# One transformer layer on one core: token sums by small products, tiles in other PSUM banks and another order of splits at the two stage changes

## The reference

```python
def rms_norm(x, g):
    xf = x.astype(jnp.float32)
    y = xf * lax.rsqrt(jnp.mean(xf * xf, axis=-1, keepdims=True) + EPS)
    return (y * g.astype(jnp.float32)).astype(x.dtype)

def modulate(h, shift, scale):
    return h * (1.0 + scale[:, None, :]) + shift[:, None, :]

        h = modulate(rms_norm(x, g_mix[i]), sh2, sc2)
        cq, ckv, kidx, widx, mq, mk, mv, ga, gb = split_cols(h @ w_in[i])
        ...
        h = modulate(rms_norm(x, g_ffn2[i]), sh3, sc3)
        x = x + 0.5 * (1.0 + gt3[:, None, :]) * swiglu(h, w1_ffn2[i], w3_ffn2[i], w2_ffn2[i])
```

## Time and profile before

| | |
|---|---|
| time, median of 3 runs | 1148.05 us (1146.92 to 1148.19) |
| profiled execution, its own time | 1148.91 us |
| its span in the profile | 1147.0 us |
| PE busy | 1121.8 us (98%) |
| DVE busy | 564.9 us (49%) |
| ACT busy | 502.2 us (44%) |
| POOL busy | 182.1 us (16%) |
| mean granted PE clock | 0.997 |

### The profile page before, as it was taken

One profiled execution on the slowest core, in us unless ns is written; L12 is line 12 of the kernel. 1 busy time (PEld: TensorE's weight loads), 2 busy tenths in 40 slices (PEclk: granted clock), 3 DMA queues, 4 the chain that ended last, 5 costly groups with the idle time before them and its releaser, 6 DMA issues.

```text
span 1147.0 us, 14769 instructions
## 1 busy us (share of the span) xinstructions
PE 1121.8 (98%) x5421; PEld 902.0 (79%) x5421; DVE 564.9 (49%) x912; ACT 502.2 (44%) x874; POOL 182.1 (16%) x114
## 2 busy tenths in 40 slices
PE   6999999999999999999999999999999999999998
PEld 4678888888888868877776778877888888888887
DVE  3544454444344475489884537677333333332232
ACT  4565646555444443244555654444232332232233
POOL 0055454454333510000000000040000000000000
PEclk9999999999999999999999999999999999999999
DMA  9846655665555333222212123322332332243221
GB/s 307 282 147 191 224 170 179 196 211 174 175 174 174 91 90 104 55 56 74 55 38 74 52 60 92 92 74 74 110 110 73 101 118 73 91 134 101 78 74 74
DMA packets 159099, 138.25 MB, mean 121 GB/s; under 512 B 3551, under 2 KB 157522, under 8 KB 159058
## 3 DMA queue, kind: packets, MB, share of 16 engines
q1 hardware_dynamic: 130948, 109.38, 30.7%
q10 hardware_dynamic: 28110, 28.32, 7.6%
HBM read 135.59 MB, written 2.10 MB: 120 GB/s over the span
## 4 chain that ended last, share of the span: by engine, by line
PE 86%; DVE 7%; SPq 3%; ACT 2%; DMA 1%; issue 1%; POOL 0%; ACTq 0%; DVEq 0%; POOLq 0%
PE ps L373 26%; PE ps L375 26%; PE ps L374 26%; SPq L926 2%; PE ps L1150 2%; PE ps L1177 2%; PE ps L1161 2%; DVE w_lo L352 2%; DVE score L1534 1%; DMA raw<-in_w_ffn 1%; DVE max L1532 1%; SPq L932 1%; DVE tmp L444 1%; ACT w_hi L347 1%; PE ps L500 1%
## 5 line engine op out<-in xcount | busy, mean ns | idle before, releaser
L352 DVE TENSOR_TENSOR w_lo<-raw,w_hi 128x1024 fp32r<-128x1024 f32 (+1 forms) x164 | 239.2, 1459 | 375.9 <-ACT w_hi L347 375.9
L373 PE MATMUL ps<-h_hi,w_hi 128*128 128x512 f32 x1008 | 400.6, 397 | 7.9 <-DVE w_lo L352 4.7
L375 PE MATMUL ps<-h_hi,w_lo 128*128 128x512 f32 x1008 | 393.7, 391 | 0.0
L374 PE MATMUL ps<-h_lo,w_hi 128*128 128x512 f32 x1008 | 393.0, 390 | 0.0
L347 ACT ACTIVATE w_hi<-raw 128x1024 fp32r<-128x1024 f32 (+1 forms) x164 | 183.5, 1120 | 362.1 <-PE ps L375 361.7
L373 PEld LDWEIGHTS ps<-h_hi,w_hi 128*128 128x128 f32 x1008 | 189.7, 188 | 54.8 <-issue 9.7
L375 PEld LDWEIGHTS ps<-h_hi,w_lo 128*128 128x128 f32 x1008 | 189.5, 188 | 40.9
L374 PEld LDWEIGHTS ps<-h_lo,w_hi 128*128 128x128 f32 x1008 | 189.9, 188 | 37.6 <-issue 0.2
L373 PE MATMUL ps<-g_hi,w_hi 128*128 128x512 f32 x330 | 129.9, 394 | 0.1
L375 PE MATMUL ps<-g_hi,w_lo 128*128 128x512 f32 x330 | 128.6, 390 | 0.0
L374 PE MATMUL ps<-g_lo,w_hi 128*128 128x512 f32 x330 | 128.5, 389 | 0.0
(11 more groups left out here) (217 smaller groups left out, 1010.6 us busy)
## 6 DMA issues: line engine op xcount, KB each, us to landing
raw<-in_w_ffn SPq DMA_DIRECT2D x42, 1024.0 KB, 5.4
ada<-in_w_ada ACTq DMA_DIRECT2D x27, 1024.0 KB, 5.1
raw<-in_w_ffn SPq DMA_DIRECT2D x16, 1408.0 KB, 6.3
raw<-in_w_in SPq DMA_DIRECT2D x64, 256.0 KB, 3.2
ada<-in_w_ada SPq DMA_DIRECT2D x16, 512.0 KB, 8.8
raw<-in_w_out SPq DMA_DIRECT2D x16, 256.0 KB, 3.0
x_tok<-in_x SPq DMA_DIRECT2D x4, 512.0 KB, 5.4
raw<-in_w_ffn SPq DMA_DIRECT2D x8, 256.0 KB, 7.3
```

The costliest lines, as they stand in the source:

```text
L352: nc.vector.tensor_tensor(tiles_of(w_lo[j % SPL], nk), raw_of(f, j, nk), tiles_of(w_hi[j % SPL], nk).bitcast(F32), ALU.subtract).then_inc( ...
L373: nc.tensor.matmul(ps[:, bank, :], hi, rhs_hi, start=start, stop=False)
L374: nc.tensor.matmul(ps[:, bank, :], hi, rhs_lo, start=False, stop=False)
L375: return nc.tensor.matmul(ps[:, bank, :], lo, rhs_hi, start=False, stop=stop)
```

## The change

It does five things, at both stage changes (n = 1 and n = 2).

1. The sums of squares are made token by token: `pe_token_sums` runs eight products of 128x1 (the partial sums as the stationary operand, a column of ones as the moving one), which leave 128x4 numbers. ACT takes their square root, DVE the reciprocal, and DVE spreads them over a diagonal of 128x512 (`dve_diag`). One product with ones (`pe_factors_and_shift`, one group later) makes the row of factors in PSUM bank 4. The scale of the mean, which stood in the squares, moves into the square root.
2. `dve_scaled` reads the factors from PSUM; a copy in `tmp[3]` (with `factor_done`) is made after the last `h_lo`, for `dve_unscale`. The copy of the shift moves there too.
3. The unscaled units go to banks 6 and 7 instead of 0 and 1. The fifth and sixth unit (banks 0 and 1) then no longer wait for the scaling. PE waits once more for the last reduction of the modulation (`ada_red`), which used these banks.
4. `pe_second_pair` runs k = 4 to 7 in blocks, too: four groups of the third unit, then four of the fourth.
5. The fifth unit's split stands at the end of `act_h` and `dve_h`, ahead of the scaling of the unscaled units. At n = 2 the sixth unit's split stands behind the first SiLU on ACT and behind the scaling on DVE.

The diff, cut to its core:

```diff
@@ -427,7 +428,7 @@
         def dve_scaled(n, k):
 
-            nc.vector.scalar_tensor_tensor(nrm[:, k % 4, :], tmp[:, 3, :] if n else ps[:, B_SUM, :], a_mul[:, n, k:k + 1], xT[:, k, :],
+            nc.vector.scalar_tensor_tensor(nrm[:, k % 4, :], ps[:, B_SUM, :], a_mul[:, n, k:k + 1], xT[:, k, :],
                                            ALU.mult, ALU.mult).then_inc(u_done, 1)
@@ -438,11 +439,9 @@
         def dve_h(dve, n, u):
 
-            dve.wait_ge(shift_psum, n)
-            nc.vector.tensor_copy(shift[:, :], ps[:, B_MOD, 0:2]).then_inc(shift_done, 1)
             dve.wait_ge(sqrt_done, n + 1)
-            nc.vector.reciprocal(tmp[:, 3, :], tmp[:, 3, :]).then_inc(rstd_done, 1)
-            dve.wait_ge(rstd_done, n + 1 + (2 if n == 2 else 0))
+            dve_diag(dve, tmp[:, 3, :], rtok[:, :], diag_done, n + 1 + (2 if n == 2 else 0))
+            dve.wait_ge(row_done, n + 1)
             dve_scaled(n, 0)
@@ -452,11 +451,16 @@
             dve_low(dve, n, KD - 1)
+            dve.wait_ge(shift_psum, n)
+            nc.vector.tensor_copy(shift[:, :], ps[:, B_MOD, 0:2]).then_inc(shift_done, 1)
+            nc.vector.tensor_copy(tmp[:, 3, :], ps[:, B_SUM, :]).then_inc(factor_done, 1)
+            lo_u(dve, u + 4)
+            dve.wait_ge(factor_done, n)
 
         def act_h(act, n, u):
 
             act.wait_ge(sum_done, n)
-            nc.scalar.activation(tmp[:, 3, :], ps[:, B_SUM, :], ACT.Sqrt, bias=eps[:, :]).then_inc(sqrt_done, 1)
+            nc.scalar.activation(rtok[:, :], ps[:, B_SUM, 0:QT], ACT.Sqrt, bias=eps[:, :], scale=1.0 / D_MODEL).then_inc(sqrt_done, 1)
@@ -471,6 +475,7 @@
                     hi_u(act, u + 3)
+            hi_u(act, u + 4)
@@ -522,12 +527,20 @@
-        def pe_sums_and_shift(pe, n):
+        def pe_token_sums(pe, n):
 
             pe.wait_ge(acc_done, 6 * n)
-            nc.tensor.matmul(ps[:, B_SUM, :], ones[:, :], tmp[:, 2, :], start=True, stop=False)
             pe.wait_ge(sq_done, KD * n)
-            nc.tensor.matmul(ps[:, B_SUM, :], ones[:, :], tmp[:, (KD - 1) % 2, :], start=False, stop=True).then_inc(sum_done, 1)
+            for t in range(QT):
+                nc.tensor.matmul(ps[:, B_SUM, t:t + 1], tmp[:, 2, t * P:(t + 1) * P], ones[:, 0:1], start=True, stop=False)
+                last = nc.tensor.matmul(ps[:, B_SUM, t:t + 1], tmp[:, (KD - 1) % 2, t * P:(t + 1) * P], ones[:, 0:1],
+                                        start=False, stop=True)
+            last.then_inc(sum_done, 1)
+
+        def pe_factors_and_shift(pe, n):
+
+            pe.wait_ge(diag_done, n + 1)
+            nc.tensor.matmul(ps[:, B_SUM, :], ones[:, :], tmp[:, 3, :], start=True, stop=True).then_inc(row_done, 1)
             pe.wait_ge(part_sum, 2 * n)
@@ -537,28 +550,30 @@
-            pe.wait_ge(x_done, KD * n + KD - 1)
+            pe.wait_ge(ada_red, 2 + (N_MOD * KD - ADA_FIRST) // 2)
...
-                    last = mm3(0, u, kk, y_hi[n][:, kk, :], y_lo[n][:, kk, :], kk == 0, kk == KD - 1)
+                    last = mm3(B_Y, u, kk, y_hi[n][:, kk, :], y_lo[n][:, kk, :], kk == 0, kk == KD - 1)
...
                 if kk == lag - 1:
-                    pe_sums_and_shift(pe, n)
+                    pe_token_sums(pe, n)
...
+                if kk == lag:
+                    pe_factors_and_shift(pe, n)
 
         def pe_second_pair(pe, n, u):
 
             half = KD // 2
-            order = [(q, k) for q in range(2) for k in range(half)] + [(q, k) for k in range(half, KD) for q in range(2)]
+            order = [(q, k0 + k) for k0 in (0, half) for q in range(2) for k in range(half)]
@@ -571,7 +586,7 @@
-                if j % 2 == 0:
+                if j % 2 == 0 and not (isinstance(i, int) and i == 1 and j == 0):
                     pe.wait_ge(g_done, KF * f + 2 * i + j // 2 + 1)
@@ -684,7 +701,11 @@
-            if not first and not unscaled:
+            if unscaled:
+                hi_u(act, U_UP[1] + 5)
+            elif f == 1 and isinstance(i, int) and i == 0:
+                pass
+            elif not first:
@@ -723,12 +744,13 @@
                 dve_unscale(dve, U_UP[1], (tmp[:, 0, :], tmp[:, 1, :]))
+                lo_u(dve, U_UP[1] + 5)
@@ -1040,7 +1062,7 @@
-                if u >= U_LAT + 4:
+                if u >= U_LAT + 6:
                     pe.wait_ge(evac, u - U_LAT - 3)
@@ -1307,7 +1329,7 @@
-                if q >= 2:
+                if q >= 3:
                     hi_u(act, u + 2)
@@ -1454,8 +1476,7 @@
-            for q in range(2, 4):
-                lo_u(dve, U_LAT + q + 2)
+            lo_u(dve, U_QKV + 1)
```

More of the change, by code:

```diff
@@ L173, in build_layer @@
         ps = ctx.enter_context(nc.psum_tensor("ps", [P, 8, SEQ], F32))
-        B_SUM, B_MOD, B_ADA = 4, 5, 6
+        B_SUM, B_MOD, B_ADA, B_Y = 4, 5, 6, 6
         U0_BANK = (6, 7, 2, 3)
@@ L225, in build_layer @@
         shift_done = sem("shift_done")
+        factor_done = sem("factor_done")
         const_done = sem("const_done")
@@ L388, in act_square @@
                 act.wait_ge(acc_done, 6 * (n - 1) + k - 1)
-            nc.scalar.activation(tmp[:, k % 2, :], xT[:, k, :], ACT.Square, scale=D_MODEL ** -0.5 if n < 3 else 1.0).then_inc(sq_done, 1)
+            nc.scalar.activation(tmp[:, k % 2, :], xT[:, k, :], ACT.Square).then_inc(sq_done, 1)
         def dve_square_sum(dve, n, k):
@@ L551, in pe_unscaled_pair @@
                     k = kk - lag
-                    last = mm3(1, u + 1, k, y_hi[n][:, k, :], y_lo[n][:, k, :], k == 0, k == KD - 1)
+                    last = mm3(B_Y + 1, u + 1, k, y_hi[n][:, k, :], y_lo[n][:, k, :], k == 0, k == KD - 1)
                     if k == KD - 1:
@@ L590, in pe_ffn @@
                 pe_second_pair(pe, 2, U_UP[f] + 2)
-            with pe.Fori(2 - f, KF // 2) as i:
+                for j in range(4):
+                    up(1, j)
+            with pe.Fori(2, KF // 2) as i:
                 for j in range(4):
@@ L717, in dve_unscale @@
                 dve.wait_ge(unit_done, done(u + q))
-                nc.vector.tensor_tensor(dst[q], ps[:, q, :], tmp[:, 3, :], ALU.mult).then_inc(y_scaled, 1)
+                nc.vector.tensor_tensor(dst[q], ps[:, B_Y + q, :], tmp[:, 3, :], ALU.mult).then_inc(y_scaled, 1)
         def dve_pair(dve, f, i, jp, nk):
@@ L730, in dve_pair @@
             else:
-                if not first:
+                if not first and not (f == 1 and isinstance(i, int) and i == 0):
                     for q in (2, 3):
```

## The result

| | before | after |
|---|---|---|
| time, median of 5 runs | 1148.11 us (1146.92 to 1148.37) | 1142.77 us (1141.8 to 1143.27) |
| span of the profiled execution | 1147.0 us | 1140.8 us |
| PE busy | 1121.8 us | 1120.4 us |
| ratio after / before | | 0.9943, 95% interval 0.9926 to 0.996 |

The changed kernel is 5.3 us faster by the medians, whose own ratio is 0.9953. By the ratio of the table it is 6.5 us faster, with an interval from 4.6 to 8.5.

A forecast was written before the change was run, and what follows sets the result against it. TensorE, busy 98% of the span, bounds the kernel, plus its stalls. Two stage changes of 25.4 us, 50.8 against 55.67, save 4.9: 1148.91 - 4.9 = 1144.0 profiled, median 1143.2 us, range 1141.8 to 1146.2.

The forecast's parts named there:

- Token sums: PE at each stage change: 16 records at 0.109 us make 1.74 us against 1.71 for two full-width sums, no gain.
- fourth rival: Small products last 0.25 us each and following products wait for the drain: slower, 1148.6 to 1150 us, chance 0.04.
- Factor: Square root, reciprocal, diagonal and row product at each stage change: scaling starts at 409.3, 1.7 us earlier.
- This wait takes the place of the reciprocal: Third tile's split waits until the first unscaled tile has ended, so the scaling chain gains only 0.3 us.
- The order in blocks: Third tile's second half runs in one block, giving the fifth tile's split 12 products (2.72 us) of cover.
- Early split ahead of scaling: Fifth tile's split precedes scaling on ACT and DVE; otherwise DVE would stand at the first tile's scaling and its copies first.
- Banks: Banks 6 and 7 free banks 0 and 1, so the fifth and sixth tiles need not wait for scaling; by themselves nothing.
- Stage time: From first unscaled product to fifth tile: 25.4 us at each stage change, together 50.8 against 55.67.
- Second rival: The wait moves to late h_lo at the third tile's last groups: 2 to 3 us gain, 1145 to 1146, chance 0.15.
- The sixth tile's split: On ACT and DVE after the first stage change: ready by 432.6, needed by PE at 433.2, margin 0.6 us.
- Profiled execution: Whole kernel: 1148.91 - 4.9 = 1144.0 us, lying 0.86 above the median, so median 1143.2.
- The first rival: The clock falls at one or both stage changes: 1144.9 us with one fall, 1146.6 with two, chance 0.12.

The follow-up runs named there:

- wide sums: Changed kernel with the full-width sums and the 128x512 square root and reciprocal, without row product and factor copy: 1144.08 us, ratio to before 0.9948.
- token sums only: Kernel before with only the token-by-token sums, the row product, the two later copies and the new ada wait: 1149.74 us, ratio to before 1.0002.
- old banks: Changed kernel with the unscaled tiles in banks 0 and 1 again and the waits that this needs: 1151.01 us, ratio to before 1.0014.
- alternating: Changed kernel, but the second half of the third and fourth tile alternates again as before: 1148.8 us, ratio to before 0.9997.
- late split: Changed kernel with the splits of the fifth and sixth tile behind the scaling again: 1148.65 us, ratio to before 0.9994.
- the kernel before with the sums apart: Kernel before with the latents' sums (24 records) cut into two halves, six full products between them: 1148.49 us, ratio to before 1.0.
- changed, sums apart: Changed kernel with the latents' sums cut into two halves, six full products between them: 1142.07 us, ratio to before 0.994.
- shift later: Changed kernel with the latents' sums in two halves and the small shift products moved to before the fourth tile: 1141.63 us, ratio to before 0.9937.
- idle filled: Kernel before with 8 and 10 unread 128x128 products where PE stands before the fifth tile: 1147.99 us, ratio to before 0.9989.

## Where the prediction was right, and the step that failed

The forecast was right in sign, and right in the mechanism at the two stage changes. It was wrong in the sum: it has no term for the clock. The gain forecast was 4.9 us. The stage times gave 4.67, and fewer clock falls gave the rest, up to 5.3 by the medians of the result, 6.2 by the spans of the two profiles and 6.5 by the ratio, which puts the time at 1141.5, below the range's low end. That the median (1142.77) still came within 0.4 us of 1143.2 is in part luck: the stage term was 0.2 us too large, and the clock term that was left out has the other sign. Step by step:

- *Token sums, "1.74 us against 1.71: nothing".* Measured 1.70. Right, and 0.109 per record holds for 32 in a row. So the fourth rival is out; its range of 1148.6 to 1150 did not follow from its own price either, at which a gain of 0.3 us was left, 1147.8.
- *Factor, "scaling starts 1.7 us earlier".* 1.73. Right.
- *"This wait takes the place of the reciprocal, and the scaling chain gains only 0.3 us".* 0.24. Right; "wide sums" and "token sums only" show it from both sides: 0.2 us at a stage change, or nothing over both.
- *"The order in blocks gives the split 12 products of cover".* Right: without it, 1.8 to 1.9 us at each change come back as the same wait of 1.79.
- *Early split ahead of scaling.* Right: 1.85 and 2.91 more without it.
- *Banks, "cost and give nothing by themselves. They free banks 0 and 1".* Right as a condition: with the old banks and the early split, PE waits 4.12 us for DVE. The banks alone, without the early split, were not run.
- *Stage time "25.4 us".* 25.53 and 25.47, so 4.67 us less where the sum has 4.9. The row product took 0.91, not 0.86, and the wait before the fourth tile was as forecast (0.29).
- *Second rival, "the wait moves" to the third tile's last groups.* It did not: in the trace after, PE is busy for all of 420 to 430 us.
- *"The sixth tile's split: ready by 432.6, PE needs it at 433.2".* It was ready at 433.38, since DVE's instruction took 2.13 us instead of 1.23. In the kernel before the same split took 1.77, too; in both, POOL runs an instruction of 128x512 beside it, and no run takes the two apart. PE needed the split at about 433.4 and went on at 433.44: the margin of 0.6 was used up, and next to nothing was lost.
- *"Profiled execution: 1148.91 - 4.9 = 1144.0. That execution lies 0.86 above the median of the runs".* This is the step that failed. The sum is made of stage times alone; it puts the change in the number of clock falls at nothing, and treats what lies between an execution and the median as a constant that both kernels share. But that distance depends on the number of falls, at 1.5 us each, and their number differs between the two kernels. The profiled execution of before had one fall, inside; the one of after had none and took 1142.77, not 1144.0. The difference of the spans, 6.15 us, is 4.67 of stage times and 1.5 of this fall. The earlier trace rows had its price already (at most 1.7); the prediction used it only against the change.
- *The first rival asked only whether the change adds a fall.* It adds none: in eight traces with the new sums no fall begins at them. It takes some away. The change puts in 1.7 us of small products and takes 1.8 and 2.3 us of idle PE out. In five traces ("alternating", "late split", "old banks", "token sums only" and the kernel before with the sums apart) a fall begins at such an idle stretch: once in its middle, three times within its last 0.5 us, once 0.5 us behind it. It does not come each time: of 13 such stretches of 1.7 to 4.1 us in seven traces, these five have a fall. The five traces of kernels without such a stretch (the changed kernel twice, "wide sums", "changed, sums apart", "shift later") have none at the stage changes, and "idle filled" shows that filling the stretches helps. The Trainium skill, "TensorE: Matmul & The Clock Gate", Part 1 (the HAM clock gate), says that the clock is set by how busy TensorE has been. The traces agree, as far as the falls begin at idle time or at long runs of small products. That the change also makes the fall behind the latents' sums rarer is not shown: the changed kernel's profiles have none there, but "wide sums", with nearly the same stage times, has one.

## What to carry to other kernels

Before a long instruction on a busy-looking engine is shortened, look for what ends the wait behind it: here a reciprocal of 3.35 us was worth 0.2, because the next split waited for a weight buffer that PE still held. Where two tiles share their product groups in turn, both end late; finishing one in a block lets its successor's preparation run under the other, but only if the preparation stands early enough in the helpers' queues and the target bank is free, and here the kernel with any one of these three taken out was no faster than before. Read the granted clock of every run before a median is taken for a sum of waits: in some executions an idle stretch costs 1.5 us more than it lasts. To check a sum of waits, compare the fastest runs of the two kernels, not only the medians: here they lie 4.66 us apart, and the stage times give 4.67.

## What the hardware showed beyond what was expected

The times of one kernel fall into steps of about 1.5 us, which go with mean granted clocks of 0.998, 0.997 and 0.995. In the traces a fall is a stretch of 3.4 us (in two places twice that, 6.8) at 1.2 GHz, and costs 1.5 us. By times and clocks the same program has such a stretch in one execution and not in another, and of the eleven traces with the same latents' sums six have one behind them. Here the falls began around products of 128x1 that ran for 2.6 to 3.5 us (from 2.6 us after their start to 1.5 us behind their end), or around an idle stretch of 1.8 us or more, but not at each of these. 18 useless products in 4.1 us of idle time (the two waits of the earlier trace rows) made a kernel 0.1% faster. When in such a place the clock does fall, and why only sometimes, no run here settles. The Trainium skill, "TensorE: Matmul & The Clock Gate", Part 1, says that the chip's look at the activity runs free of the kernel's start; the spread between executions of one kernel agrees with that, but no trace here shows it.
